# Three order changes around a post-norm and a linear-attention entry: when two small loads are issued, who fills zeros, and where VectorE's adds and row products stand

## The reference, cut to what matters

```python
for i in range(DEPTH_3):                       # 4 layers: i % 3 picks the mixer
    xn = rms_norm(h, norm_gains[i, 0])
    if kind == 0:   m = stick_breaking_mixer(...)   # layers 0 and 3
    elif kind == 1: m = short_conv_mixer(...)       # layer 1
    else:           m = gla_mixer(...)              # layer 2, gated linear attention
    h = h + rms_norm(m, norm_gains[i, 1])      # post-norm behind the mixer
    f = squared_relu_mlp(rms_norm(h, norm_gains[i, 2]), ffn_w_up[i], ffn_w_down[i])
    h = h + rms_norm(f, norm_gains[i, 3])      # post-norm behind the MLP
```

## Time and profile before

| | |
|---|---|
| time, median of 3 runs | 2759.99 us (2758.69 to 2762.76) |
| time of the profiled execution | 2770.17 us |
| its span, first to last instruction | 2768.3 us |
| TensorE busy | 2706.8 us (98%) |
| VectorE, ScalarE, GpSimd busy | 68%, 45%, 23% |
| mean granted TensorE clock | 0.991 of 2.4 GHz |

### The profile page before, as it was taken

The page is one execution under the profiler, slowest core; times in us unless marked ns, Lnnn a source line. Parts: engine busy times, 40 slices in busy tenths (PEclk is TensorE's granted clock), DMA queues, the critical chain, the costliest instruction groups (busy, mean ns, idle before and its releaser), DMA issues.

```text
span 2768.3 us, 43691 instructions
## 1 busy us (share of the span) xinstructions
PE 2706.8 (98%) x17285; PEld 2401.8 (87%) x17285; DVE 1878.1 (68%) x2051; ACT 1246.4 (45%) x1594; POOL 634.1 (23%) x519
## 2 busy tenths in 40 slices
PE   8999999999999999999999999999999999999998
PEld 7997789999979999998799888888888878888887
DVE  6875765588777886655666657666766767665765
ACT  4443454444444444445444454444444454445443
POOL 5963400078536861000100100000000420000000
PEclk9999999999999999999999999999999999999999
DMA  7754145567527766534355435435653436533552
GB/s 287 264 207 156 47 168 200 187 229 280 192 83 256 268 227 236 182 123 137 136 200 188 155 105 230 188 122 200 224 199 122 154 131 228 200 132 108 212 206 91
DMA packets 127001, 502.04 MB, mean 181 GB/s; under 512 B 11168, under 2 KB 12480, under 8 KB 93488
## 3 DMA queue, kind: packets, MB, share of 16 engines
q1 hardware_dynamic: 112768, 450.40, 45.7%
q0 software_dynamic: 14128, 50.18, 5.2%
HBM read 499.48 MB, written 1.06 MB: 181 GB/s over the span
## 4 chain that ended last, share of the span: by engine, by line
PE 86%; DVE 7%; ACT 3%; issue 2%; DMA 1%; POOL 1%; SPq 0%; DVEq 0%; ACTq 0%; POOLq 0%
PE duo L1271 8%; PE duo L1256 8%; PE duo L1257 8%; PE duo L1254 7%; PE duo L1401 7%; PE duo L1409 7%; PE duo L1405 7%; PE duo L1270 4%; PE duo L1764 3%; PE duo L1765 3%; PE duo L1769 3%; DVE in_lo L373 2%; DVE down_lo L373 1%; ACT in_hi L366 1%; PE duo L2309 1%
## 5 line engine op out<-in xcount | busy, mean ns | idle before, releaser
L373 DVE TENSOR_TENSOR in_lo<-ring_in,in_hi 128x2048 fp32r<-128x2048 f32 x295 | 691.9, 2346 | 346.5 <-ACT in_hi L366 345.9
L366 ACT CAST in_hi<-ring_in 128x2048 fp32r<-128x2048 f32 (+1 forms) x293 | 556.0, 1898 | 247.6 <-PE duo L1769 132.1
L373 DVE TENSOR_TENSOR down_lo<-ring_down,down_hi 128x1024 fp32r<-128x1024 f32 (+1 forms) x196 | 350.0, 1786 | 29.2 <-ACT down_hi L366 29.2
L1518 ACT CAST hid_hi<-act 128x256 fp32r<-128x256 f32 (+1 forms) x196 | 93.4, 476 | 418.3 <-DVE act L1604 347.9
L366 ACT CAST down_hi<-ring_down 128x1024 fp32r<-128x1024 f32 (+1 forms) x196 | 260.6, 1329 | 44.2 <-PE duo L1409 44.2
L1401 PE MATMUL duo<-down_hi,hid_hi 128*128 128x512 f32 x928 | 242.8, 393 | 7.1 <-ACT hid_hi L1518 7.0
L1254 PE MATMUL duo<-feat,in_hi 128*128 128x512 f32 x1024 | 246.5, 392 | 0.0
L1256 PE MATMUL duo<-feat,in_hi 128*128 128x256 f32 (+1 forms) x1015 | 240.5, 280 | 3.4 <-ACT in_hi L366 3.4
L1409 PE MATMUL duo<-down_hi,hid_lo 128*128 128x512 f32 x928 | 239.4, 390 | 0.3 <-DVE hid_lo L1591 0.3
L1405 PE MATMUL duo<-down_lo,hid_hi 128*128 128x512 f32 x928 | 239.5, 390 | 0.0
L1257 PE MATMUL duo<-feat,in_hi 128*128 128x256 f32 x1015 | 239.3, 279 | 0.0
(11 more groups left out here) (532 smaller groups left out, 5632.9 us busy)
## 6 DMA issues: line engine op xcount, KB each, us to landing
ring_in<-in_ffn_in SPq DMA_DIRECT2D x196, 1024.0 KB, 6.7
ring_down<-in_ffn_down SPq DMA_DIRECT2D x132, 512.0 KB, 3.8
ring_down<-in_ffn_down SPq DMA_DIRECT2D x64, 1024.0 KB, 4.9
mod_w<-in_w_ada POOLq DMA_DIRECT2D x72, 512.0 KB, 5.4
ring_in<-in_sb_w_qkv SPq DMA_DIRECT2D x24, 1024.0 KB, 5.1
ring_in<-in_conv_w_in SPq DMA_DIRECT2D x12, 1024.0 KB, 5.0
ring_in<-in_gla_w_in SPq DMA_DIRECT2D x12, 1024.0 KB, 5.1
ring_in<-in_nsa_w_in SPq DMA_DIRECT2D x10, 1024.0 KB, 5.2
```

The source lines that it names most:

```text
L366: act.copy(hi[:, s, 0:n], raw[:, s, 0:n]).then_inc(hi_ready.sem, 1)
L373: dve.tensor_tensor(lo[:, s, 0:n], raw[:, s, 0:n], hi[:, s, 0:n].bitcast(F32), ALU.subtract).then_inc(lo_ready.sem, 1)
```

## The change

It has five edits. (1) The two loads of `GlaIn` are issued by GpSimd ahead of the four small operations of the `Feed` before it, once all four adds are done, and no longer behind them. (2) The zeros of `kf` are written by two copies on ScalarE, between its cast of a weight unit and its cast of `w_low`, and no longer by GpSimd. (3) In a post-norm behind a `Linear`, VectorE adds up the sums ahead of the row products of half 0, and makes the first diagonal ahead of the last two products. (4) In the others, the second mean stands ahead of the third product and both diagonals ahead of the fourth. (5) In all seven, the two adds of half n = 0 move from behind the adds of half 1 into `late_lo`, behind the low half of the unit `late`.

```diff
@@ Feed.gpsimd
+        if self.early_loads:
+            self.early_loads(pool)
         pool.wait_ge(k.squares_ready.sem, self.s0 + 1)
         pool.wait_ge(k.squares_dve_ready.sem, self.q0 + 1)
@@ PostNorm.late_lo
         if self.feeds.late is not None:
             in_lo(self.k, dve, self.feeds.late)
+        for t in range(TT):
+            self._add(dve, t, 0)
@@ PostNorm._vector_by_part
+        from_rows = isinstance(self.feeds, Linear)
         for t in range(TT):
             dve.wait_ge(k.acc_squared.sem, self.sq0 + t + 1)
-            self._times_row(dve, t)
             self._part(dve, t)
+            if not from_rows:
+                self._times_row(dve, t)
         dve.wait_ge(k.acc_squared.sem, self.sq0 + 3)
         self._mean(dve, 0)
-        self._times_row(dve, 2)
+        if from_rows:
+            self._times_row(dve, 0)
+            self._times_row(dve, 1)
+            self._diagonal(dve, 0)
         dve.wait_ge(k.acc_squared.sem, self.sq0 + 4)
         self._mean(dve, 1)
+        self._times_row(dve, 2)
+        for t in range(int(from_rows), TT):
+            self._diagonal(dve, t)
         self._times_row(dve, 3)
-        for t in range(TT):
-            self._diagonal(dve, t)
         for c in range(4):
             self.follow.lo(dve, c)
         dve.wait_ge(k.acc_times_row.sem, self.z0 + 4)
-        for n in (1, 0):
-            for t in range(TT):
-                self._add(dve, t, n)
+        for t in range(TT):
+            self._add(dve, t, 1)
@@ GlaIn.__init__
+        before.early_loads = self._loads
@@ GlaIn.scalar
         in_hi(k, act, u + 2)
+        zeros = k.c("causal", 0, P).unsqueeze(1).broadcast_to([P, 8, P])
+        for i in range(2):
+            act.copy(self.kf[i].rearrange("p (a n) -> p a n", n=P), zeros).then_inc(self.cleared, 1)
         act.wait_ge(self.landed, self.landed0 + 32)
         act.copy(self.low_hi, self.w_low).then_inc(self.low_hi_ready, 1)
@@ GlaIn.gpsimd, its first lines now in GlaIn._loads
-    def gpsimd(self, pool):
+    def _loads(self, pool):
         k = self.k
         wait_all(pool, self.feeds.before)
         pool.dma_start(self.w_low...).then_inc(self.landed, 16)
         pool.dma_start(self.w_up[0:16, :], ...).then_inc(self.landed, 16)
-        for i in range(2):
-            pool.memset(self.kf[i], 0.0).then_inc(self.cleared, 1)
+
+    def gpsimd(self, pool):
+        k = self.k
         pool.wait_ge(self.cleared, 2)
```

More of the change, by code:

```diff
@@ L597, in __init__ @@
         self.turns_late = True
+        self.early_loads = None
         spare = isinstance(before, Linear)
```

## The result

The changed kernel takes 2782.24 us (median of 7 runs, 2776.26 to 2785.24); the kernel before took 2762.42 us beside it on the same chip (7 runs, 2757.83 to 2771.49). The two medians lie 19.8 us apart. The ratio that the runs give, by which the rest of the text goes, is 1.0063, with a 95% interval from 1.0052 to 1.0074: 17.4 us slower, between 14 and 20. The profiled execution took 2785.24 us, 15.07 more than the one of before.

The account below looks back on a forecast made before the run. The prediction took TensorE to bound the kernel, busy for 2706.8 of 2768.3 us. Its terms, 15.5 - 0.8 - 1.0 + 6.7 = +20.4 us, took the median from 2759.99 to 2780.4 us, range 2768 to 2786.

Parts of the forecast that it names:

- four waits ahead of an MLP: At L1401, four places: third add delays ScalarE's casts and VectorE's low half by 2.58 us; each wait 1.42 becomes 4.0.
- two projections: Short convolution and second stick-breaking attention: low half of the next unit 2.58 us late, all of it lost by TensorE.
- diagonals behind mixers: At L652, four places: first diagonal comes sooner, gain 0.2 us each (between 0 and 0.36), 0.8 in all.
- linear attention: At its entry: early loads and no GpSimd fills bring the 16 columns' low half sooner; gain 1.0 us, bounds 0 and 1.68.
- clock: Behind the four stops ahead of an MLP: one clock fall each at 1.67 us, 6.7 in all, bounds 0 and 6.7.
- starting the second half's splits sooner: Behind a mixer: moving the adds brings no gain there; the rival with splits 1.36 us earlier gave 2765.5 us, chance 0.07.
- The rival with the clock held: At the new stops: they come but the clock grant stays 1.00; +13.7 us, 2773.7 us, chance 0.22.
- a rule of the Trainium skill's page: At the linear attention: GpSimd excludes VectorE's two-port-pair scalings, but early loads don't slow VectorE's squares; gain 1.0 us, not 0.
- Not slower: At MLPs and projections: TensorE has work queued, the six delays cost nothing; -1.8 us, 2758.2 us, chance 0.07.

Follow-up runs that it names:

- experiment 1: The changed kernel with all four adds ahead of the feature splits again, so all edits but the postponed adds: 2758.65 us, ratio 0.9984 to the kernel before.
- experiment 2: The kernel before with only the two adds postponed: 2784.33 us, ratio 1.0083 to the kernel before.
- 10: The changed kernel with both sums of squares moved behind the first unit of each of the four MLPs: 2764.42 us, ratio 0.9997 to the kernel before.
- experiment 4: The changed kernel with only the add of tile 1 postponed, that of tile 0 early again: 2766.56 us, ratio 1.0022 to the kernel before.
- Experiment 5: The changed kernel with adds postponed only ahead of the three mixers, early again ahead of the MLPs: 2763.44 us, ratio 0.9993 to the kernel before.
- experiments 3: The changed kernel with six constant products on TensorE in each of the four stops ahead of an MLP: 2772.06 us, ratio 1.0035 to the kernel before.
- experiment 6: The kernel before with only the key buffers' zeros moved from GpSimd's fills to copies on ScalarE: 2765.47 us, ratio 1.0007.
- 7: The kernel before with only the two loads issued early, zeros still on GpSimd behind the norm: 2762.01 us, ratio 0.9992.

## Why the prediction was right, and where it wasn't

The direction, the mechanism and the size of the total held: +20.4 us forecast, +17.4 (14 to 20) measured. From the last point that the change can't have touched (TensorE's L2172 of the stick-breaking attention, 1648.38 us before and 1642.46 after) to the end, the two profiled executions differ by 15.1 + 5.9 = 21.0 us. The terms, in those executions:

| term | forecast | measured | from |
|---|---|---|---|
| four waits ahead of an MLP | +10.3 | +10.7 | 16.4 - 5.7 |
| two projections | +5.2 | +1.4 | L2319, 1.43 |
| diagonals behind mixers | -0.8 | -1.4 | waits gone |
| linear attention | -1.0 | -0.35 | 1.68 to 1.33 |
| clock | +6.7 | +10.1 | the stretches above |
| sum | +20.4 | +20.5 | |

The total is closer than its terms: a term that was too large and one that was too small made up for each other, and that is luck.

**Ahead of an MLP: right.** The chain is the one foretold: third add, ScalarE's sum, its next cast, VectorE's low half, TensorE. The delay was 2.70 us where 2.58 was worked out. Experiments 1 and 2 tie it to the adds, 10 to ScalarE's place in the chain, and 4 gives the part that is VectorE's own (0.78 for one add). Of the 2.70 us, 1.16 are VectorE's wait for ScalarE's cast; without that wait its own way, with the two adds, would still have been 1.54 us later than before. That nothing was gained by starting the second half's splits sooner was right too: VectorE has its features no earlier and waits 1.28 us for them in the changed kernel.

**"The same ahead of a projection": the step that failed.** It put 2.58 us on each of two projections. It took the product at 1869.94 for the first one of the next weight unit. It is the first product of the last tile of the unit in hand: a block is four tiles of some 2.7 us, and in the trace of before the tiles begin at 1864.40, 1867.22 and 1869.94, with the low half's products at the end of each. So the low half that ended at 1871.75 wasn't used at 1871.76: that was the old unit's. The products of the new unit come later in the trace of before:

```profile
1872.66 0.39 PE L1764 MATMUL duo<-in_hi,feat 128*128 128x512 f32 x1
...
1874.47 1.07 PE L1769 MATMUL duo<-in_lo,feat 128*128 128x512 f32 x4
```

Its low half was ready 2.72 us ahead of its first use, so a delay of 2.58 us just fits. In the trace after, the new unit begins at 1871.95, and its high half was there 0.64 us sooner; the low half was there 0.13 us before its first product. Experiment 5 puts the price of all three entries of a mixer at about 2.5 us. The 1.4 us that did come, at the second stick-breaking attention, fall on a later unit, whose cast on ScalarE waited for a load (`ring_in`). A late issue of that load alone doesn't make the wait: in experiment 2 it was issued as late (8.3 us behind the start of the late low half, as in the changed kernel), landed 5.3 us later, and TensorE didn't wait. In the changed kernel it took 7.0 us, and in experiments 3, 5 and 10, which have the wait too, 7.2 to 7.4. Why it took longer there stays open.

**The clock: the right mechanism, with a bound that didn't hold.** The term had one fall of 3.7 us at 0.55 per stop as its price and its upper bound. In the profiled execution of the changed kernel the low level lasted about twice as long behind three of the four stops, which makes 10.1 us in place of 6.7. In that of experiment 2, with stops of the same length, it was short four times and cost 6.8, which is the forecast's term. One execution of each doesn't say how often either comes. Experiment 3 measures over many executions: 7.7 us, give or take 5, which fits both. The rival with the clock held came to pass only there, where TensorE was given work: 9.7 us above before, and not the rival's 13.7, mainly because that had the two projections in full. The Trainium skill's page "TensorE: Matmul & The Clock Gate", section "HAM oscillation — how this bites in real kernels", lets the array start at half rate each time behind a gap that recurs at each stage; the traces agree for the four stops of 4.1 us, and in experiment 4 for only two of the four of 2.2 us.

**Diagonals: the gain was at its upper bound.** All of the 0.36 us went, four times.

**Linear attention: the right pieces, the wrong last one.** The diagonals came down to 0.48 us as foretold. But the forecast let the loads land 4.70 us behind their issue, at 2153.3, well before VectorE's low half. In the change they landed 5.27 behind it, and the cast waited 1.34 us for them, so the gain is 0.35 and not 1.0. The step had reckoned with the adds ahead of these loads, and put the first issue 3.64 us behind the start of the late low half; it came 3.90 behind it. What it had wrong is mainly the landing, which it took from one execution: the same two loads took 3.37 us in experiment 2 and 4.69 in experiment 6, and what sets it was not tried. Without the postponed adds the loads start sooner and the whole wait of 1.68 us goes (experiment 1).

The step also weighed a rule of the Trainium skill's page "SBUF — State Buffer", section "Who interferes with whom", on GpSimd and VectorE. The traces agree with what it says of the scaling: the scaled identities are held while GpSimd works (0.92 and 1.91 us in experiments 6 and 7, 0.48 where it rests). VectorE's squares beside the early loads aren't held (1.23 us, from 1.22), as the forecast took from it; whether GpSimd reads SBUF during an issue, on which the rule would turn, no run here shows.

**Not slower,** the rival with work in hand, was right for the short convolution, where TensorE had 2.72 us of work in hand, and wrong for the MLPs. The wait of 1.42 us that stood against it was evidence for the MLPs alone.

## What to carry to other kernels

An operation moved out of the way of one engine is paid for by what waits for its result on another: here the adds cost VectorE little, but ScalarE's program has a sum behind the third add and a cast behind the sum. Before pricing a delay at a stop that isn't in the list of waits, count the products between the late operand's unit and the unit in hand; a single matching time is no proof of use. Work whose result isn't needed soon (here the sums of squares) belongs behind the first operand that the bottleneck needs, and moving them there took 4.6 us off TensorE's waits here.

## What the hardware showed that was not expected

Stops of the same length have different ends: of four stops of 2.2 us in one execution, two were followed by the low clock (8 products in 3.54 and 3.65 us) and two not (2.08 and 2.09), a stop of 2.40 us before left it alone, and one of 1.83 us in experiment 5 didn't. What besides the length decides was not tried. Behind the stops of 4.1 us the low level lasted some 3 us once and some 7 us three times in the changed kernel, and some 3 us four times in experiment 2. And GpSimd's issue of a DMA holds VectorE's scaled identity as its fills do: the pair took 0.92 us beside the issue of 0.97, and 0.48 alone.
